# Banded scores: the product with the keys' rest on 64 partitions a head, two heads side by side in the array

## The reference

```python
q = q.reshape(bsz, nb, BLOCK, SWA_KV_HEADS, SWA_G, HEAD_DIM)
...
kb, vb = band(k), band(v)            # blocks n-1, n, n+1: 384 keys
sc = jnp.einsum('bnqkgd,bnjkd->bnkgqj', q, kb).astype(jnp.float32) * (HEAD_DIM ** -0.5)
...
sc = jnp.where(valid[None, :, None, None], sc + bias, NEG)
m = jnp.maximum(jnp.max(sc, axis=-1, keepdims=True), sink_l)
e = jnp.exp(sc - m)
p = e / (jnp.sum(e, axis=-1, keepdims=True) + jnp.exp(sink_l - m))
o = jnp.einsum('bnkgqj,bnjkd->bnqkgd', p.astype(vb.dtype), vb)
```

## Time and profile before

| what | value |
|---|---|
| median of 3 runs | 2293.96 us (2293.66 to 2296.55) |
| the profiled execution | 2296.69 us, span 2294.9 us |
| mean granted clock of PE | 0.994 |
| PE busy | 2218.7 us, 97% of the span |
| PEld busy | 1856.6 us, 81% |
| DVE busy | 1619.7 us, 71% |
| ACT busy | 1008.8 us, 44% |
| POOL busy | 533.0 us, 23% |

### The profile page before, as it was taken

How to read it: one execution, slowest core, us unless ns; L and a number is a source line. 1 busy time by engine, 2 the same in 40 slices (tenths; PEclk the granted TensorE clock), 3 DMA queues, 4 the chain that set the end, 5 groups by cost and what they waited for, 6 DMA issues and landing times.

```text
span 2294.9 us, 29127 instructions
## 1 busy us (share of the span) xinstructions
PE 2218.7 (97%) x11410; PEld 1856.6 (81%) x11410; DVE 1619.7 (71%) x2047; ACT 1008.8 (44%) x1789; POOL 533.0 (23%) x308
## 2 busy tenths in 40 slices
PE   6999999999999999999999999999999999999998
PEld 5888887888888888788888888778888888877877
DVE  4399776884449987787545998678644698867853
ACT  3333324772333333576342333368633334336841
POOL 1212133221112222322112222223211212323210
PEclk9999999999999999999999999999999999999999
DMA  4211111015111111103411111100422111110012
GB/s 158 66 45 42 37 42 47 1 56 193 69 61 43 46 38 42 37 10 103 149 62 65 38 43 37 50 28 19 147 102 83 38 45 42 37 42 28 29 65 92
DMA packets 38807, 136.34 MB, mean 59 GB/s; under 512 B 4720, under 2 KB 5232, under 8 KB 38672
## 3 DMA queue, kind: packets, MB, share of 16 engines
q1 hardware_dynamic: 38672, 134.47, 17.1%
HBM read 116.63 MB, written 17.83 MB: 59 GB/s over the span
## 4 chain that ended last, share of the span: by engine, by line
PE 85%; DVE 7%; ACT 3%; POOL 2%; issue 2%; DMA 0%; SPq 0%; POOLq 0%; ACTq 0%
PE ps L523 45%; PE ps L774 14%; PE ps L723 6%; PE ps L758 4%; PE ps L738 4%; PE ps L576 2%; PE ps L602 2%; PE ps L590 2%; DVE accC L1329 1%; PE ps L533 1%; PE ps L280 1%; DVE PTb L1248 1%; DVE cat L1541 1%; DVE bnb L1516 1%; PE ps L753 1%
## 5 line engine op out<-in xcount | busy, mean ns | idle before, releaser
L523 PE MATMUL ps<-hT,stat 128*128 128x512 f32 x4416 | 1057.6, 393 | 1.1 <-POOL stat L836 1.1
L523 PEld LDWEIGHTS ps<-hT,stat 128*128 128x128 f32 x4416 | 816.8, 188 | 165.5 <-POOL stat L836 3.3
L836 POOL TENSOR_TENSOR stat<-raw,stat 128x1024 fp32r<-128x1024 f32 x92 | 250.1, 2719 | 936.4 <-ACT stat L965 936.4
L1329 DVE SCALAR_TENSOR_TENSOR accC<-uC,parT,accC 128x1024 f32<-128x1024 f32 x240 | 421.2, 1792 | 2.6
L774 PE MATMUL ps<-woR,catR 128*128 128x512 f32 x1536 | 354.9, 391 | 9.1 <-POOL catR L852 9.1
L774 PEld LDWEIGHTS ps<-woR,catR 128*128 128x128 f32 x1536 | 287.9, 189 | 69.1 <-POOL catR L852 9.9
L1516 DVE TENSOR_REDUCE bnb<-ps 128x1 f32<-128x1024 f32 x128 | 156.2, 1221 | 55.8 <-PE ps L723 55.1
L1248 DVE TENSOR_TENSOR PTb<-ps,PTb 128x512 fp32r<-128x512 f32 x256 | 163.4, 679 | 19.1 <-ACT PTb L1141 18.1
L1141 ACT ACTIVATE PTb<-ps 128x512 fp32r<-128x512 f32 x256 | 138.9, 595 | 69.6 <-PE ps L738 66.8
L1133 ACT ACTIVATE Pb<-ps,bnb 128x1024 f32<-128x1024 f32 x128 | 143.1, 1118 | 46.4 <-DVE bnb L1516 44.5
L758 PE MATMUL ps<-PTb,Vb 128*128 128x256 f32 x1024 | 155.7, 296 | 0.0
(11 more groups left out here) (192 smaller groups left out, 2844.3 us busy)
## 6 DMA issues: line engine op xcount, KB each, us to landing
raw<-w_in SPq DMA_DIRECT2D x100, 512.0 KB, 3.5
y<-xs SPq DMA_DIRECT2D x32, 512.0 KB, 2.6
raw<-w_out SPq DMA_DIRECT2D x24, 512.0 KB, 3.5
xs<-x SPq DMA_DIRECT2D x16, 512.0 KB, 3.5
xs<-y SPq DMA_DIRECT2D x16, 512.0 KB, 3.5
xd<-x SPq DMA_DIRECT2D x8, 512.0 KB, 10.3
ropeT<-rope SPq DMA_DIRECT2D x4, 1024.0 KB, 5.7
rawX<-w_out SPq DMA_DIRECT2D x8, 512.0 KB, 4.1
```

The source lines that it names most:

```text
L523: last = mm(ps[:, 2 * (c % 2) + h, :], w[:, a, k, :], hT[:, h, b, k, :], start=(k == 0 and (a, b) == (0, 0)), stop=(k == KD - 1 and (a, b) ...
L836: pool.tensor_tensor(dst[:, 1], src, dst[:, 0].bitcast(F32), ALU.subtract).then_inc(q["wlo"], 1)
L1329: last_tap[j] = conv.add(stt(accC[:, j, :], uC[:, j, t:t + T], w, accC[:, j, :], ALU.mult, ALU.add))
```

## The change

In `d_scores` the loops over the heads and the parts change places, so that a unit makes part 0 of both heads and then part 1 of both. Part 0 keeps its 128 partitions. Part 1 takes only the 64 partitions of the head's main part, the lower half for g = 0 and the upper for g = 1: query main times key rest; query rest times key rest is left out of the sum. The two products of part 1 lie in different halves of the array's rows and write to different banks. The number of products and loads stays four a unit.

```diff
-                        for g in range(2):
-                            h = 2 * kv + g
-                            for part in range(2):
-                                last = mm(ps[:, 4 + g, 0:nk * P], Qst[:, h, n * P:(n + 1) * P],
-                                          Kst[kv][part][:, k0 * P:(k0 + nk) * P], start=(part == 0), stop=(part == 1))
+                        for part in range(2):
+                            for g in range(2):
+                                h = 2 * kv + g
+                                r = slice(0, P) if part == 0 else slice(HD * g, HD * g + HD)
+                                last = mm(ps[:, 4 + g, 0:nk * P], Qst[r, h, n * P:(n + 1) * P],
+                                          Kst[kv][part][r, k0 * P:(k0 + nk) * P], start=(part == 0), stop=(part == 1))
                         last.then_inc(q["ds_mm"], 1)
```

## The result

The changed kernel takes 2302.65 us (median of 11 runs, 2299.27 to 2306.78), the kernel before in the same comparison 2293.96 (11 runs, 2291.56 to 2297.69). The ratio is 1.0037, 95% interval 1.0028 to 1.0046: slower by 8.5 us, 6.4 to 10.6.

What follows compares the result with a forecast made beforehand. PE was taken to bound the score stage. Per unit, 0.41 us for row changes, less 0.178 or 0.118 saved, plus 0.055, summed to 19.3 us over 64 units: 2313.3 us from 2294.0, range 2308 to 2321.5.

Steps and rivals of the forecast that it cites:

- PE bounds the stage: In the four stretches of banded scores, PE was taken as the bound, busy for 950.6 of 952 us.
- Step (1): Reordering a unit's score products, both heads' first part and then both heads' second, was costed at nothing.
- Fewer rows alone cost nothing: Claim from 96-row products in group B's scores, which follow 128-row ones at their pace, 0.23 us each.
- 0.41 us for the two changes: Price per unit of going to 64 rows and back to 128, 0.205 us each; 26.2 us over 64 units.
- 0.055 us for the second product of the pair: Time the second 64-row product still adds, half a load interval of 0.11 us; ends kept at 0 and 0.178.
- the pair costs what one costs: Rival: the second 64-row product disappears beside the first; 15.8 us slower, 2309.8 us; chance 0.25.
- Nothing hides it: Each unit's two row changes are paid in full, as PE is the stage's bound and its order fixed; 26.2 us.
- The clock: Rival: clock falls behind column sums in all twelve such units, adding 19 us; 2332 us; chance 0.04.
- What is late next: Unit's signal comes 0.08 us later, but later work has room; PE's 0.4 us reciprocal wait at L599 stays unchanged.
- Serial pair: Rival: the two 64-row products run one behind the other, nothing saved; 26.2 us slower, 2320.2 us; chance 0.12.
- lower to upper half as a change: Rival: going from lower to upper half costs another 0.205 us per unit, 13.1 us; 2333.3 us; chance 0.04.
- no price at all: Rival: no change of rows is paid in the score units, saving 10.4 us; 2283.6 us; chance 0.05.

Runs made afterwards that it cites:

- e_reorder: Changed kernel with all score products back on 128 rows, so only their order differs from the kernel before; 2294.12 us, ratio 1.0002 to the kernel before.
- e_rows96: Kernel before with the second part of the even heads' scores on 96 partitions; 2295.51 us, ratio 1.0006 to the kernel before.
- e_pad: Kernel before with the last score product of each unit made twice, all with 128 rows; slower than before by 7.1 us (4.6 to 9.9).
- e_pad_same: Kernel before with each unit's last score product made twice, three times in four units of a pass, all 128 rows; slower by 6.7 us (4.1 to 9.2).

## Why the prediction was wrong, point by point

- **PE bounds the stage: right.** 203.66 of 203.66 us after the change.
- **Step (1) costs nothing: right** (e_reorder). **Fewer rows alone cost nothing: right** (e_rows96).
- **0.41 us for the two changes: a little high.** In place they take 0.385, just under the 0.39 to which its doubt of 0.02 reached; 64 x 0.025 = 1.6 us too much. The column sums of the earlier trace rows, which it used only as a check, were nearer: 0.19 for the way in, or 0.38 for both.
- **0.055 us for the second product of the pair: the first step that failed.** It takes nothing: the two start within 0.01 us. The rows of before gave the load's interval for the same rows only, and I took half of it as the doubt's middle. By their start times the second adds 0.003 us, 52 ns less than taken, 64 x 0.052 = 3.3 us. For this term the rival "the pair costs what one costs" was right, and the Trainium skill's rule beside it ("TensorE: Matmul & The Clock Gate", Part 3: about 4 ns between the starts of two tiles in different row groups) agrees with this trace, at 0.003 us. With both terms right the sum of PE order is 48 x 0.207 + 16 x 0.266 = 14.2 us (from the first score product to the second projection product). That alone gives 2308.2 us, still at the lower end of the range; the next two points took the time out of it.
- **"Nothing hides it": the second step that failed, by 2 us.** The stage and the last units grew by 12.2. Part of the difference can be seen in the first unit of a pass. In the kernel before, the projection load behind it waited for the weights' rest, split on POOL:

```profile
658.10 0.53 PEld L523 LDWEIGHTS ps<-hT,stat 128*128 128x128 f32 x3 [0.17 <-POOL stat L836]
```

  In the changed kernel the unit's way out covers that wait, and this unit grows by 0.05 us instead of 0.27, 0.9 us over the passes. The rest is some 0.02 us a unit, and its cause stays open.
- **The clock: right as a place to look, wrong in its sign, and the third step that failed.** I had it only as a rival that costs more, and left the falls of the kernel before in both sides of the sum as if they stayed. Some three falls fewer gave about 4 us back, a term that the sum put at nothing. The whole account is 19.3 - 1.6 - 3.3 - 2.2 - 3.7 = 8.5, where the last term is what is left over, and the falls fit it.
- **What is late next: right.** PE's waits outside the stage are the same; the wait for the reciprocal (now at L600) is 1.6 us over the four passes, 0.4 a pass as in the earlier trace rows.
- **The rivals.** Serial pair, lower to upper half as a change, and no price at all: all three are refuted by the profile after. The rule of the Trainium skill ("TensorEngine Tiling (Array Packing)", Key Properties: changing the tiling mode drains the TensorE) agrees with the runs: each change is paid, at about 0.19 us.

## What to carry to other kernels

Before two half-height products are put side by side, count the ways in and out: here each change between 128 and 64 rows cost 0.19 us of PE order, and a pair of 384 columns gives back 0.175, so one pair in a visit loses, two came out even, and it should take three to gain (an estimate; no run here puts three pairs in the place of six full products). Find the price in the profile by the loader's idle time ahead of a load of another height, and measure the gain of a pair by itself. Where the difference is below half a per cent, count the falls of the clock in each trace before the rest of a sum is believed: three falls more or fewer are 4 to 5 us, and here they hid a third of the work added.

## What the runs showed of the hardware

- Two loads into different row halves start together and take 0.19 us together; two into the same half take 0.29.
- A change of rows costs the same at 256 and 384 columns (0.387 and 0.384 us for both ways) and is paid each time (four a unit: 0.76 us). With 96 rows there is none.
- The number of falls to the lower clock was different from kernel to kernel (2 to 11 in a trace) and from run to run of one kernel (2, 4 and 6 in the changed one), and each made the span about 1.55 us longer. With 128-row products alone added to the scores it was 8 in one trace (e_pad, its slowest run) and 2 in another (e_pad_same).
